# Activation-table preloads, norm order, scratch buffers and one-hot copies rearranged in an eight-core encoder step

## The chip, the cores and the metric

The kernel runs on all eight cores of one Trainium2 chip, each core on its own eighth of the tokens, with no exchange between cores. The time is that of the slowest core in device microseconds, from one launch. A profile shows one execution on its slowest core: TensorE (PE, with its weight loads PEld), VectorE (DVE), ScalarE (ACT), GpSimd (POOL, which only issues the weight loads here) and SyncE (SP, which issues the other transfers). PEclk is the granted TensorE clock, 1.00 for 2.4 GHz and 0.50 for 1.2 GHz.

## The reference

Two layers of a streaming encoder. Layer 0 mixes tokens by a convolution module, layer 1 by grouped-query attention with a relative-position bias; each layer ends with a SwiGLU block. Every block reads a modulated RMSNorm of the residual stream.

```python
for i in range(DEPTH):
    mod = jax.nn.silu(c) @ p['w_mod'][i] + p['b_mod'][i]
    sh1, sc1, g1, sh2, sc2, g2 = jnp.split(mod, 6, axis=-1)
    h = modulate(rms_norm(x, p['norm_mix'][i]), sh1, sc1)
    ...                                   # conv_module (i = 0) or attention (i = 1) -> y
    x = x + g1[:, None, :] * y
    h = modulate(rms_norm(x, p['norm_ffn'][i]), sh2, sc2)
    x = x + g2[:, None, :] * swiglu(h, p['w_gu'][i], p['w_down'][i])
return rms_norm(x, p['norm_out']), ...

def modulate(h, shift, scale):
    return h * (1 + scale[:, None, :]) + shift[:, None, :]

# bias of attention: bucket of (key position - query position), one table of 32 buckets x 32 heads
b = jnp.take(table.astype(jnp.float32), bucket, axis=1)
```

## The kernel before

Channels lie on the 128 partitions in 16 chunks (KC), tokens on the free axis (1184 columns X, in three tiles of 384, 384 and 416; from attention on 1056 columns in three tiles of 352). The last tile also holds the 2 x 16 sample tokens, which have their own modulation, so each modulated write of it is three instructions (384 or 320, 16 and 16 columns). All weights stream through a ring of four 1 MB slots (`RING`): POOL issues a load when TensorE has released a slot.

The order on every engine is the order in which the Python code emits it; engines wait for each other by semaphores. The stages in order: norm and modulation blocks, pw1 with the convolution, pw2 (its first three weight blocks as a head that goes chunk by chunk), FFN 0, k/v projection, the attention bias, attention with the q projections, output projection wo, FFN 1, final norm.

**Norm.** While the last projection before a norm runs, ACT squares each finished chunk and TensorE sums the squares with a matrix of ones into PSUM. Then `rstd1(t)` makes 1/rms of tile t: one Ln and one Exp on ACT. `rstd` calls it for tile 0, `rest` for tiles 1 and 2. `apply(t, c0, c1)` writes the modulated norm HB chunk by chunk: DVE multiplies X by 1/rms into one of three scratch buffers `T1`, then ACT (Identity with scale and bias) or DVE itself (`tensor_scalar`, chunks with c % 5 == 4, in tile 2 also c % 5 == 1) writes HB. A buffer is free again when that second step is done.

**FFN head.** TensorE starts gate and up of the first three weight blocks on tile 0, chunk by chunk as HB comes, into six PSUM banks. `evac` empties a pair: Silu on ACT into a scratch buffer `SGF` (two), multiply on DVE. Tiles 1 and 2 follow on the same three blocks; their `apply` calls stand between the evacuations in the code, so ACT and DVE do them in that order. Only after tile 2 of a block is its ring slot released.

**k/v projection.** The same chunk-by-chunk form for three tiles, on the same PSUM banks, so a tile can start only when `k_evac` (ACT) and `v_evac` (DVE) of the tile before are done. Part of the next tile's `apply` stands before these evacuations, the rest behind. After the last apply, `load_consts` loads caches and one-hot tables into space that X held.

**Attention bias.** 18 units; 16 of them first copy a shifted one-hot window (96 x 2048 bf16) into one of two buffers `OHW`, then TensorE does 16 small matmuls with it, then DVE adds the mask. After each unit TensorE does half a tile of the first q projection (8 matmuls of 352 columns); after every second half ACT evacuates the tile. The copies alternate between ACT and DVE, and each is issued one unit ahead (`oh_build(u + 1)` behind the matmuls of unit u).

**Tables.** `table(func)` is a one-element activation into `DUM`. ACT holds the functions of one table set at a time; the compiler puts an ACT_TABLE_LOAD straight in front of an activation whose function is not there. The nine calls stand where the next function is not needed yet.

Of the kernel before, what the change touches and what calls it, by code (L numbers as in the profile page):

```python
# [13 lines left out]
KC = 16  # L14
# [66 lines left out]
def build_nc():  # L81
# [44 lines left out]
    with es:  # L126
# [18 lines left out]
        EPSC = sb("EPSC", (128, 1), F32)  # L145
        DUM = sb("DUM", (128, 1), F32)
        BDW = sb("BDW", (128, 128), F32)
# [20 lines left out]
        XP = carve(UBraw, 9728, (128, KC, 32), F32)  # L168
        SGF = carve(SCR, 0, (128, 2, 416), F32)
        RSTD = carve(SCR, 3328, (128, NX), F32)  # L170
# [4 lines left out]
        T1U = carve(UBraw, 4736, (128, 3, 416), F32)  # L175
        YS = carve(UBraw, 4736, (128, 4, NQ), F32)
# [225 lines left out]

        def table(func):
            act(DUM[:], EPSC[:], func)

        sqf = [None, None, None]
        SB = (2, 4, 5)

        class Norm:
            def __init__(self, tiles):  # L410
                self.tiles = tiles
                self.k = 0
                self.pend = []
                self.cn = [0, 0, 0]
                self.ready = {}
                self.rtok = {}
                self.t1f = [None] * 3
                self.tk = 0
# [33 lines left out]
            def rstd(self, R, T, li, which):  # L452
                self.flush(0)
                self.R, self.T, self.li, self.which = R, T, li, which
                if which is not None:
                    tam = am_calc(li, which, 0, KC)
                    ACT.wait(tam)
                    DVE.wait(tam)
                    self.hb = {}
                self.rstd1(0)  # L460

            def rest(self):
                self.rstd1(1)
                self.rstd1(2)

            def apply(self, t, c0=0, c1=KC):
# [4 lines left out]
                for c in range(c0, c1):  # L471
                    i = self.tk % 3
                    self.tk += 1
                    Tc = self.T[:, i, :]
                    DVE.wait(self.t1f[i])
                    DVE.emit(nc.vector.tensor_tensor(out=Tc[:, 0:ncols], in0=X[:, c, xlo:xlo + ncols],  # L476
                                                     in1=self.R[:, xlo:xlo + ncols], op=ALU.mult))
                    td = DVE.tick()
                    if c % 5 == 4 or (t == 2 and c % 5 == 1):
                        DVE.wait(td)  # L480
                        for (a, b_, bi) in segs(xlo, xlo + ncols):
                            DVE.emit(nc.vector.tensor_scalar(
                                out=HB[:, c, 32 + a:32 + b_], in0=Tc[:, a - xlo:b_ - xlo], scalar1=AM[:, c, bi:bi + 1],
                                scalar2=MOD[:, li, sh0 + c, bi:bi + 1], op0=ALU.mult, op1=ALU.add))
# [86 lines left out]
        def ffn(li, tiles, nm, nm2):  # L571
            ngrp = (NFF + GRP - 1) // GRP
            sgf = [None] * 2
            st = {"kk": 0, "dk": 0, "sg": 0}

            def evac(j, t, bg, bu, tpg, tpu):
                xlo, ncols = tiles[t]
                aslot = (j // GRP % 2) * GRP + j % GRP
                i = st["sg"] % 2
                st["sg"] += 1  # L580
# [52 lines left out]
            for G in range(ngrp):  # L633
# [430 lines left out]
        t_bv = dma(SP, BVB, bkv_d.partition_broadcast(128), ldc_sem)  # L1064
        nm2.apply(0, 0, 3)
        nm2.rest()
        nm2.apply(0, 3, KC)
        table(AF.Exp)
        DVE.emit(nc.vector.memset(V1[:].rearrange("p v (g d) -> p v g d", d=65)[:, :, :, 64:65], 1.0))
        for t in range(3):  # L1070
# [463 lines left out]
```

How the kernel before makes its waits and increments, by code:

```python
    def tick(self):  # L61
        if not self.marked:
            self.n += 1
            self.last.then_inc(self.sem, 1)
            self.marked = True
        return (self.sem, self.n)
# [1 line left out]
    def wait(self, *ts):  # L68
        for t in ts:
            if t is None:
                continue
            sem, v = t
            if v <= 0:
                continue
            k = id(sem)
            if self.seen.get(k, 0) >= v:
                continue
            self.e.wait_ge(sem, v)
            self.seen[k] = v
# [166 lines left out]
        def dma(engw, out, in_, sem):  # L246
            engw.e.dma_start(out=out, in_=in_).then_inc(sem, 16)
            cnt[id(sem)] = cnt.get(id(sem), 0) + 1
            return (sem, 16 * cnt[id(sem)])
```

## Time and profile before

| | |
|---|---|
| Profiled execution, time | 3382.72 us |
| its span on the slowest core | 3381.0 us |
| spans of the eight cores | 3332.6 to 3381.0 us |
| three runs, median (lowest to highest) | 3572.45 us (3382.72 to 3860.07) |
| busy: PE / DVE / ACT / POOL | 2986.7 / 1147.8 / 708.6 / 187.2 us |
| mean granted clock of that core | 0.959 |

The profiled execution is the lowest of the three runs, and all durations below are its own. A line of the timeline is: start, duration, engine, source line, instruction, tiles and shapes, count of merged instructions, and in brackets how long the engine had been idle and on whom it waited. All TensorE instructions come from one helper, L252, all activations from L255; stages are told apart by tile names (SCR holds T1, SGF and the squares; UBraw holds T1 of the k/v norm and QT; Xraw holds X, and during attention the bias and one-hot tiles).

### The profile page before, as it was taken

The page shows a single profiled execution, that of the slowest core. Times are in us where ns is not written, and L with a number is a line of the kernel's source. Part 1 is how long each engine was busy: PE and PEld are TensorE (multiplying, and loading weights), DVE is VectorE, ACT ScalarE, POOL GpSimd, SP SyncE. Part 2 cuts the span into 40 slices and gives each one's busy share as a digit, 9 for nine tenths or more (in the row PEclk, how much of TensorE's full clock was granted, in tenths as well). Part 3 has the DMA queues.
Part 4 walks back from the last instruction along what each step waited for, and adds up shares of the span by engine and source line. Part 5 has one row for each costly group of instructions (what it writes and reads, how often), then busy time and mean ns, then how long its engine had stood idle before and what let it go on. Part 6 is the DMA issues. An engine that isn't in the chain of part 4 may idle for free.

```text
span 3381.0 us, 54942 instructions; the slowest of 8 cores (3332.6 to 3381.0 us)
## 1 busy us (share of the span) xinstructions
PE 2986.7 (88%) x21988; PEld 1855.3 (55%) x21988; DVE 1147.8 (34%) x2680; ACT 708.6 (21%) x1342; POOL 187.2 (6%) x357
## 2 busy tenths in 40 slices
PE   2299774688999999999999879889999999999996
PEld 0166453354556555565555447655556666666663
DVE  0345444614141221414122656633222222222236
ACT  2411111555000000000000556655200000000003
POOL 0000000000000000000000000000000000000000
PEclk9999886898999999999999989989999999999998
DMA  9789988593856566574523738653465253535243
GB/s 216 134 158 180 149 151 172 130 180 53 135 101 113 96 111 115 91 126 87 99 44 66 170 55 140 124 141 63 83 118 100 48 92 55 94 51 99 45 76 120
DMA packets 107976, 370.52 MB, mean 110 GB/s; under 512 B 31520, under 2 KB 51104, under 8 KB 78784
## 3 DMA queue, kind: packets, MB, share of 16 engines
q0 software_dynamic: 51024, 285.67, 49.4%
q1 hardware_dynamic: 56704, 81.34, 8.7%
q8 instruction: 180, 2.95, 0.4%
q14 instruction: 68, 0.56, 0.1%
HBM read 615.89 MB, written 33.78 MB: 192 GB/s over the span
## 4 chain that ended last, share of the span: by engine, by line
PE 77%; DMA 11%; DVE 5%; ACT 3%; issue 2%; SPq 1%; POOL 0%; DVEq 0%; ACTq 0%; POOLq 0%
PE ps L252 77%; DMA UBraw<-ud 2%; DMA ud<-UBraw 2%; ACT HBraw L255 1%; DMA Xraw<-xT 1%; SPq L247 1%; DMA RING<-wgu 1%; DMA RING<-wmod 1%; DMA zd<-UBraw 1%; ACT SCR L255 1%; DVE SCR L476 1%; DMA RING<-wpw 1%; DVE Xraw L663 1%; DVE Xraw L965 1%; DMA SCR<-bkv 0%
## 5 line engine op out<-in xcount | busy, mean ns | idle before, releaser
L252 PE MATMUL ps<-HBraw,RING 128*128 128x352 bf16 (+2 forms) x11616 | 1935.6, 327 | 84.9 <-ACT SCR L255 26.6
L252 PEld LDWEIGHTS ps<-HBraw,RING 128*128 128x128 bf16 x11616 | 1135.7, 99 | 815.3 <-issue 123.3
L252 PE MATMUL ps<-UBraw,RING 128*128 128x352 bf16 (+2 forms) x4992 | 813.9, 320 | 14.6 <-DVE UBraw L585 6.4
L252 PEld LDWEIGHTS ps<-UBraw,RING 128*128 128x128 bf16 x4992 | 472.8, 98 | 332.1 <-issue 64.6
L585 DVE TENSOR_TENSOR UBraw<-ps,SCR 128x352 bf16<-128x352 f32 (+2 forms) x264 | 144.2, 547 | 1181.5 <-PE ps L252 1172.6
L255 ACT ACTIVATE SCR<-ps 128x352 f32<-128x352 f32 (+2 forms) x264 | 127.0, 482 | 1823.7 <-PE ps L252 1822.9
L663 DVE SCALAR_TENSOR_TENSOR Xraw<-ps,MOD,Xraw 128x16 f32<-128x16 f32 (+3 forms) x960 | 395.3, 447 | 321.8 <-PE ps L252 321.8
L252 PE MATMUL ps<-SCR,ONESB 128*128 128x352 bf16 (+2 forms) x240 | 77.5, 363 | 84.6 <-ACT SCR L255 84.6
L252 PE MATMUL ps<-SCT,RING 128*128 128x3 bf16 x3072 | 90.6, 165 | 65.3 <-ACT HBraw L255 45.5
L252 PEld LDWEIGHTS ps<-SCT,RING 128*128 128x128 bf16 x3072 | 90.5, 97 | 78.0 <-issue 68.7
L255 ACT ACTIVATE SCR<-Xraw 128x352 bf16<-128x352 f32 (+2 forms) x190 | 107.5, 568 | 104.0 <-DVE Xraw L513 55.5
L252 PE MATMUL ps<-UBraw 128*128 128x156 bf16 x640 | 56.1, 257 | 69.3 <-DMA UBraw<-ud 66.9
L513 DVE TENSOR_TENSOR Xraw<-Xraw,SCR 128x352 f32<-128x352 f32 (+2 forms) x78 | 42.3, 542 | 182.7 <-ACT SCR L255 182.7
L247 POOL DMA_DIRECT2D RING<-wmod x96 | 50.9, 531 | 942.1 <-PE ps L252 932.2
L255 ACT ACTIVATE Xraw<-Xraw 128x512 bf16<-128x512 f32 (+4 forms) x146 | 93.2, 656 | 42.9 <-DVE Xraw L1243 34.8
L247 POOL DMA_DIRECT2D RING<-wdn x96 | 50.7, 528 | 861.2 <-PE ps L252 843.0
L247 POOL DMA_DIRECT2D RING<-wgu x88 | 46.5, 529 | 890.3 <-PE ps L252 887.6
L255 ACT ACTIVATE SCR<-ps,G1B,MOD 128x384 f32<-128x384 f32 (+3 forms) x160 | 79.1, 536 | 76.5 <-PE ps L252 64.0
L252 PEld LDWEIGHTS ps<-UBraw 128*128 128x128 bf16 x640 | 53.8, 110 | 72.7 <-issue 71.3
L1243 DVE SCALAR_TENSOR_TENSOR Xraw<-ps,Xraw 128x512 f32<-128x512 f32 x128 | 82.2, 685 | 31.4 <-PE ps L252 31.3
L252 PEld LDWEIGHTS ps<-SCR,ONESB 128*128 128x128 bf16 x240 | 23.3, 102 | 117.4 <-issue 109.4
L255 ACT ACTIVATE SCR<-UBraw 128x32 bf16<-128x32 f32 (+3 forms) x50 | 32.0, 639 | 245.2 <-DVE UBraw L857 190.6
(93 smaller groups left out, 1074.6 us busy)
## 6 DMA issues: line engine op xcount, KB each, us to landing
RING<-wmod POOLq DMA_DIRECT2D x96, 1024.0 KB, 13.2
RING<-wgu POOLq DMA_DIRECT2D x88, 1024.0 KB, 9.2
RING<-wdn POOLq DMA_DIRECT2D x80, 512.0 KB, 5.3
RING<-wpw POOLq DMA_DIRECT2D x24, 1024.0 KB, 17.1
Xraw<-xT SPq DMA_DIRECT2D x26, 592.0 KB, 11.9
RING<-wqkv POOLq DMA_DIRECT2D x10, 1024.0 KB, 14.3
zd<-UBraw SPq DMA_DIRECT2D x16, 592.0 KB, 10.1
Xraw<-zd SPq DMA_DIRECT2D x16, 592.0 KB, 7.6
```

Source lines behind the costliest of these rows:

```text
L247: engw.e.dma_start(out=out, in_=in_).then_inc(sem, 16)
L252: return PE.emit(nc.tensor.matmul(out, lhsT=lhsT, rhs=rhs, start=start, stop=stop, **kw))
L255: return ACT.emit(nc.scalar.activation(out=out, in_=in_, func=func, **kw))
L476: DVE.emit(nc.vector.tensor_tensor(out=Tc[:, 0:ncols], in0=X[:, c, xlo:xlo + ncols], in1=self.R[:, xlo:xlo + ncols], op=ALU.mult))
L513: DVE.emit(nc.vector.tensor_tensor(out=dst[:, xlo:xlo + ncols], in0=dst[:, xlo:xlo + ncols], in1=TMPE[:, 0:ncols], op=ALU.add))
L585: DVE.emit(nc.vector.tensor_tensor(out=ACTR[:, aslot, xlo:xlo + ncols], in0=PS[bu][:, 0:ncols], in1=SGF[:, i, 0:ncols], op=ALU.mult))
L663: DVE.emit(nc.vector.scalar_tensor_tensor(out=X[:, n, a:b_], in0=PS[bk][:, a - xlo:b_ - xlo], scalar=MOD[:, li, 80 + n, bi_:bi_ + 1], in1= ...
L965: DVE.emit(nc.vector.tensor_tensor(out=zt, in0=zt, in1=mv, op=ALU.subtract))
L1243: DVE.emit(nc.vector.scalar_tensor_tensor(out=SS[:, 2 * w + half, :], in0=bank[:, :], scalar=0.125, in1=BIAS[:, 8 * a + 2 * ip + half, :], ...
```

## The change

It touches five things; weights, matmuls and transfers stay, and the orders of PE, POOL and SP are the same row for row.

1. The nine `table` calls go.
2. `rest` goes: `rstd` makes 1/rms of all three tiles before the first `apply`.
3. `T1` has two buffers instead of three, `SGF` three instead of two. DVE writes HB itself for chunks with c % 4 == 3 in every tile.
4. The cuts of `apply` are moved: 8 and 8 chunks around the evacuations in FFN (10 and 6 before) and in k/v (3 and 13 before).
5. All one-hot copies go to ACT, and each is issued in its own unit, not one ahead.

```diff
-        T1 = carve(SCR, 8064, (128, 3, 416), F32)
+        T1 = carve(SCR, 9728, (128, 2, 416), F32)
-        SGF = carve(SCR, 0, (128, 2, 416), F32)
+        SGF = carve(SCR, 0, (128, 3, 416), F32)
-        def table(func):
-            act(DUM[:], EPSC[:], func)
...
-                self.rstd1(0)
-            def rest(self):
-                self.rstd1(1)
-                self.rstd1(2)
+                for t in range(3):
+                    self.rstd1(t)
...
-                    i = self.tk % 3
+                    i = self.tk % 2
...
-                    if c % 5 == 4 or (t == 2 and c % 5 == 1):
+                    if c % 4 == 3:
...
-            nm.apply(0, 0, 3)
-            nm.rest()
-            nm.apply(0, 3, KC)
-            table(AF.Silu)
+            nm.apply(0)
...
-            nm.apply(1, 0, 10)
+            nm.apply(1, 0, 8)
             for j in range(3):
                 evac(j, 0, hbk[j][0], hbk[j][1], tp, tp)
-            nm.apply(1, 10, KC)
+            nm.apply(1, 8, KC)
...
             if t < 2:
-                nm2.apply(t + 1, 0, 3)
+                nm2.apply(t + 1, 0, 8)
...
-                nm2.apply(t + 1, 3, KC)
+                nm2.apply(t + 1, 8, KC)
...
-        def oh_build(u):
-            t, qg, x = u // 9, u % 9, ohs.index(u) % 2
...
-            if x:
-                DVE.wait(ohfree[x])
-                DVE.emit(nc.vector.tensor_copy(out=dst, in_=src))
-                oh_t[u] = DVE.tick()
-            else:
-                ACT.wait(ohfree[x])
-                act(dst, src, AF.Copy)
-                oh_t[u] = ACT.tick()
         def bias_unit(u):
...
             if qg < 8:
-                PE.wait(oh_t[u])
+                ACT.wait(ohfree[u % 2])
+                act(OHW[0:96, u % 2, :, :].rearrange("r q (p i) -> r q p i", p=8), src, AF.Copy)
+                PE.wait(ACT.tick())
...
-            if u + 1 in ohs:
-                oh_build(u + 1)
```

What stands in ACT's queue at the start of FFN 0, before (SCR<-ps,EPSC is an Ln, SCR<-SCR its Exp, HBraw<-SCR an apply, DUM the preload of Silu, SCR<-ps a Silu):

```order
L255 ACTIVATE SCR<-ps,EPSC 128x384
L255 ACTIVATE SCR<-SCR 128x384
L255 ACTIVATE HBraw<-SCR,MOD,AM 128x384 x3
L255 ACTIVATE SCR<-ps,EPSC 128x384
L255 ACTIVATE SCR<-SCR 128x384
L255 ACTIVATE SCR<-ps,EPSC 128x416
L255 ACTIVATE SCR<-SCR 128x416
L255 ACTIVATE HBraw<-SCR,MOD,AM 128x384 x10
L255 ACTIVATE DUM<-EPSC 128x1
L255 ACTIVATE HBraw<-SCR,MOD,AM 128x384 x8
L255 ACTIVATE SCR<-ps 128x384 x3
L255 ACTIVATE HBraw<-SCR,MOD,AM 128x384 x5
```

The same place in the changed kernel:

```order
L254 ACTIVATE SCR<-ps,EPSC 128x384
L254 ACTIVATE SCR<-SCR 128x384
L254 ACTIVATE SCR<-ps,EPSC 128x384
L254 ACTIVATE SCR<-SCR 128x384
L254 ACTIVATE SCR<-ps,EPSC 128x416
L254 ACTIVATE SCR<-SCR 128x416
L254 ACTIVATE HBraw<-SCR,MOD,AM 128x384 x18
L254 ACTIVATE SCR<-ps 128x384 x3
L254 ACTIVATE HBraw<-SCR,MOD,AM 128x384 x6
```

Two Ln and Exp pairs moved from behind the third apply to ahead of the first, the preload is gone, and six instead of eight applies of tile 1 stand before the Silus.

ACT's queue in the attention bias, before (Xraw<-Xraw 96x2048 is a one-hot copy, UBraw<-ps the evacuation of a q tile):

```order
L255 ACTIVATE Xraw<-Xraw 96x2048 x2
L255 ACTIVATE UBraw<-ps,VTs 128x352
L255 ACTIVATE Xraw<-Xraw 96x2048
L255 ACTIVATE UBraw<-ps,VTs 128x352
L255 ACTIVATE Xraw<-Xraw 96x2048
L255 ACTIVATE UBraw<-ps,VTs 128x352 x2
```

and in the changed kernel:

```order
L254 ACTIVATE Xraw<-Xraw 96x2048 x2
L254 ACTIVATE UBraw<-ps,VTs 128x352
L254 ACTIVATE Xraw<-Xraw 96x2048 x2
L254 ACTIVATE UBraw<-ps,VTs 128x352
L254 ACTIVATE Xraw<-Xraw 96x2048 x2
```

Two copies now stand between two evacuations where one stood; the other eight copies left DVE's queue.

## Rows read from the trace of the kernel before

**Rows 1.** The page, part 4: the chain that ended last, by engine.
```profile
PE 77%; DMA 11%; DVE 5%; ACT 3%; issue 2%; SPq 1%; POOL 0%; DVEq 0%; ACTq 0%; POOLq 0%
```

**Rows 2.** Windows: length, busy us (instructions) of each engine, PEclk, DMA share, GB/s.
```profile
786.00:836.00 50.00, 39.23 (x209) 20.89 (x209) 34.97 (x77) 36.06 (x70) 0.00 (x0) 0.88 0.12 22
1925.00:1987.00 62.00, 42.40 (x272) 24.45 (x272) 38.62 (x96) 42.38 (x84) 7.70 (x14) 0.86 0.47 95
1987.00:2019.00 32.00, 24.11 (x387) 17.62 (x388) 17.85 (x33) 16.18 (x14) 0.53 (x1) 0.87 0.48 91
2347.00:2395.00 48.00, 37.04 (x209) 21.12 (x210) 32.64 (x77) 33.91 (x70) 0.00 (x0) 0.87 0.10 20
```

**Rows 3.** Groups by line and form: count, busy us, mean ns, idle before.
```profile
L255 ACT ACTIVATE UBraw<-ps,VTs 128x352 bf16<-128x352 f32 x48 | 26.3, 548 | 31.0 <-PE ps L252 31.0
...
L255 ACT ACTIVATE Xraw<-Xraw 96x2048 bf16<-96x2048 bf16 x8 | 15.2, 1903 | 5.8 <-DMA UBraw<-cv 3.9 <-PE ps L252 1.9
...
L255 ACT ACT_TABLE_LOAD x10 | 12.8, 1283 | 25.4 <-DMA FLAG<-flag 14.2 <-DVE UBraw L939 9.7 <-PE ps L252 1.4
...
L1130 DVE COPY Xraw<-Xraw 96x2048 bf16<-96x2048 bf16 x8 | 5.8, 722 | 0.0
L482 DVE TENSOR_SCALAR HBraw<-SCR,AM,MOD 128x384 bf16<-128x384 f32 x12 | 5.7, 479 | 1.3
```

**Rows 4.** Timeline of ACT before pw2: LayerNorm statistics, then its application.
```profile
583.83 1.28 ACT L255 ACT_TABLE_LOAD   x1 [9.67 <-DVE UBraw L939]
...
591.44 0.71 ACT L255 ACTIVATE HBraw<-Xraw,VTs 128x384 bf16<-128x384 f32 x1 [0.43 <-DVE Xraw L967]
```

**Rows 5.** Timeline, start of FFN 0: 1/rms, first applies, first matmuls.
```profile
786.67 0.52 ACT L255 ACTIVATE SCR<-SCR 128x384 f32<-128x384 f32 x1
...
787.95 1.90 ACT L255 ACTIVATE HBraw<-SCR,MOD,AM 128x384 bf16<-128x384 f32 x3 [0.76 <-DVE SCR L476]
...
788.94 17.31 PE L252 MATMUL ps<-HBraw,RING 128*128 128x384 bf16 x96 [2.76 <-DVE SCR L476]
...
789.76 0.56 ACT L255 ACTIVATE SCR<-ps,EPSC 128x384 f32<-128x384 f32 x1
...
791.98 1.29 ACT L255 ACTIVATE HBraw<-SCR,MOD,AM 128x384 bf16<-128x384 f32 x2
```

**Rows 6.** Timeline, FFN 0 head: applies, first Silus, restarts of TensorE.
```profile
795.65 2.61 DVE L476 TENSOR_TENSOR SCR<-Xraw,SCR 128x384 f32<-128x384 f32 x5
796.30 2.50 ACT L255 ACTIVATE HBraw<-SCR,MOD,AM 128x384 bf16<-128x384 f32 x4 [0.61 <-DVE SCR L476]
...
807.06 0.84 ACT L255 ACTIVATE SCR<-ps 128x384 f32<-128x384 f32 x2
...
808.39 4.79 PE L252 MATMUL ps<-HBraw,RING 128*128 128x384 bf16 x15 [2.14 <-DVE UBraw L585]
...
814.02 14.73 PE L252 MATMUL ps<-HBraw,RING 128*128 128x384 bf16 x89 [0.83 <-ACT HBraw L255]
...
835.80 14.48 PE L252 MATMUL ps<-HBraw,RING 128*128 128x416 bf16 x70 [0.45 <-ACT HBraw L255]
```

**Rows 7.** Timeline, k/v: evacuation of tile 0, last apply, constants (POOL), first copy.
```profile
1940.87 2.35 ACT L255 ACTIVATE SCR<-ps,VTs 64x384 bf16<-64x384 f32 x4
...
1965.90 3.77 ACT L255 ACTIVATE HBraw<-UBraw,MOD,AM 128x384 bf16<-128x384 f32 x9 [0.96 <-DVE UBraw L476]
...
1970.28 4.11 POOL L247 DMA_DIRECT2D SCR<-ckT  x8 [51.44 <-ACT HBraw L255]
...
1985.14 1.91 ACT L255 ACTIVATE Xraw<-Xraw 96x2048 bf16<-96x2048 bf16 x1 [3.93 <-DMA UBraw<-cv]
```

**Rows 8.** Timeline, attention bias: a unit, its q matmuls, first matmuls of attention.
```profile
2004.12 0.55 PE L252 MATMUL ps<-Xraw 96*128 96x32 bf16 x16 [1.00 <-ACT Xraw L255]
...
2004.53 1.35 PE L252 MATMUL ps<-HBraw,RING 128*128 128x352 bf16 x8
...
2018.45 1.87 PE L252 MATMUL ps<-UBraw,SCR 128*128 128x256 bf16 x8 [1.48 <-DVE Xraw L1165]
```

More of the change, by code:

```diff
@@ L145, in build_nc @@
         EPSC = sb("EPSC", (128, 1), F32)
-        DUM = sb("DUM", (128, 1), F32)
         BDW = sb("BDW", (128, 128), F32)
@@ L168, in build_nc @@
         XP = carve(UBraw, 9728, (128, KC, 32), F32)
-        SGF = carve(SCR, 0, (128, 2, 416), F32)
-        RSTD = carve(SCR, 3328, (128, NX), F32)
-        T1 = carve(SCR, 8064, (128, 3, 416), F32)
+        SGF = carve(SCR, 0, (128, 3, 416), F32)
+        RSTD = carve(SCR, 4992, (128, NX), F32)
+        T1 = carve(SCR, 9728, (128, 2, 416), F32)
         SQ = carve(SCR, 13056, (128, 3, 416), BF16)
@@ L174, in build_nc @@
         RSTDU = carve(UBraw, 0, (128, NX), F32)
-        T1U = carve(UBraw, 4736, (128, 3, 416), F32)
+        T1U = carve(UBraw, 4736, (128, 2, 416), F32)
         YS = carve(UBraw, 4736, (128, 4, NQ), F32)
@@ L416, in __init__ @@
                 self.rtok = {}
-                self.t1f = [None] * 3
+                self.t1f = [None, None]
                 self.tk = 0
@@ L572, in ffn @@
             ngrp = (NFF + GRP - 1) // GRP
-            sgf = [None] * 2
+            sgf = [None] * 3
             st = {"kk": 0, "dk": 0, "sg": 0}
@@ L578, in evac @@
                 aslot = (j // GRP % 2) * GRP + j % GRP
-                i = st["sg"] % 2
+                i = st["sg"] % 3
                 st["sg"] += 1
@@ L643, in ffn @@
                 last = G == ngrp - 1
-                if last:
-                    table(AF.Ln)
                 PE.wait(DVE.tick())
@@ L706, in build_nc @@
         trs = ACT.tick()
-        table(AF.Sigmoid)
         DVE.wait(trs, t_ld)
@@ L946, in build_nc @@
         tstat = ACT.tick()
-        table(AF.Silu)
         DVE.wait(tstat)
@@ L1064, in build_nc @@
         t_bv = dma(SP, BVB, bkv_d.partition_broadcast(128), ldc_sem)
[L1065 to L1068, printed above, removed]
+        nm2.apply(0)
         DVE.emit(nc.vector.memset(V1[:].rearrange("p v (g d) -> p v g d", d=65)[:, :, :, 64:65], 1.0))
@@ L1118, in build_nc @@
         ohfree = [None, None]
-        ohs = [u for u in range(18) if u % 9 < 8]
-        oh_t = {}
-        def oh_build(u):
-            t, qg, x = u // 9, u % 9, ohs.index(u) % 2
-            src = OHP[0:96, qg, :, 0:16]
-            src = bass.AP(src.tensor, src.offset + 15 + 16 * t, [list(src.ap[0]), [-1, 16], [48, 8], [1, 16]])
-            dst = OHW[0:96, x, :, :].rearrange("r q (p i) -> r q p i", p=8)
-            if x:
-                DVE.wait(ohfree[x])
-                DVE.emit(nc.vector.tensor_copy(out=dst, in_=src))
-                oh_t[u] = DVE.tick()
-            else:
-                ACT.wait(ohfree[x])
-                act(dst, src, AF.Copy)
-                oh_t[u] = ACT.tick()
         def bias_unit(u):
@@ L1141, in bias_unit @@
             if qg < 8:
-                PE.wait(oh_t[u])
+                src = OHP[0:96, qg, :, 0:16]
+                src = bass.AP(src.tensor, src.offset + 15 + 16 * t, [list(src.ap[0]), [-1, 16], [48, 8], [1, 16]])
+                ACT.wait(ohfree[u % 2])
+                act(OHW[0:96, u % 2, :, :].rearrange("r q (p i) -> r q p i", p=8), src, AF.Copy)
+                PE.wait(ACT.tick())
             PE.wait(*bf[bk])
@@ L1145, in bias_unit @@
                 if qg < 8:
-                    oh = OHW[0:96, ohs.index(u) % 2, q, :]
+                    oh = OHW[0:96, u % 2, q, :]
                 else:
@@ L1151, in bias_unit @@
             if qg < 8:
-                ohfree[ohs.index(u) % 2] = tp
-            if u + 1 in ohs:
-                oh_build(u + 1)
+                ohfree[u % 2] = tp
             DVE.wait(tp)
@@ L1200, in build_nc @@
         gq = q_dense(0)
-        oh_build(0)
         for u in range(18):
@@ L1374, in build_nc @@
         nm4.rstd(RSTDU, T1U, 1, None)
-        nm4.rest()
         y_t = [None] * 4
```

2 lines of the change are left out of this document (removed).

## The prediction, as it was put on record

> **What bounds the kernel now.** I read the chain of waits first: TensorE holds 77% of it [rows 1], so work on ACT and DVE costs nothing except where TensorE waits for it. So I looked next for the stretches where it does, in the windows: the starts of the two FFNs, the k/v projection and the attention bias. There TensorE is busy 39 of 50, 37 of 48, 42 of 62 and 24 of 32 us, at a granted clock of 0.86 to 0.88 [rows 2]. The edits that are not free lie in these 192 us; the timelines of the stretches give the price. In the FFN start the reader should see three restarts of TensorE: at 788.94 behind the first apply, at 808.39 behind the first Silu, and at 814.02 and 835.80 behind the last applies of tiles 1 and 2 [rows 5, 6].
>
> **Table preloads.** A load takes 1.28 us, and there are ten [rows 3]. In the order of the code the functions change Silu, Ln, Sigmoid, Ln, Silu, Ln, Silu, Ln, Exp, Ln, Silu, Ln; that gives ten loads if Exp needs none behind Ln, nor Ln behind Exp, so the preloads of Exp and of Ln before FFN 1 load nothing, and on demand the same ten remain. A load without a preload begins only when the wait of its activation is over: at 583.83 ACT had stood 9.67 us for DVE, and then loaded [rows 4]. So each load whose activation heads the chain costs 1.28 us: the Ln of 1/rms at FFN 0, k/v and the final norm, and the first Silu of both FFN heads. Two others cost nothing. The Silu of pw2's LayerNorm falls on its first chunk, but a chunk there takes ACT 0.71 us of a cycle of 0.71 + 0.43 that DVE sets [rows 4], so ACT has made up 1.28 us after three chunks; without that slack it costs 1.28. The Sigmoid of pw1 is hidden while TensorE fills the other pair of banks (32 matmuls, over 5 us at the 0.166 us each of [rows 6]).
>
> The Trainium skill (ScalarE: Activation LUTs, What ACT_TABLE_LOAD costs) adds a drain of about 1.38 us to each load, 2.66 us in all. The trace shows only 1283 ns, and the load at 583.83 starts with ACT already idle; by the page these five loads would make the sum below 7 us longer.
>
> **FFN 0 head.** (a) The first apply begins after ACT's Exp, which ends at 787.19, and after DVE's multiply. In the change two Ln and Exp pairs stand ahead of it; from 789.76 to 791.98 they take 2.22 us [rows 5]. Behind the load ACT is free at about 787.1 + 1.28 + 2.22 = 790.6 instead of starting at 787.95: **+2.65**. TensorE's 96 matmuls follow by as much, if the applies keep up.
>
> (b) Do they, with two T1 buffers? Before, five chunks take ACT 2.50 + 0.61 us [rows 6], 0.62 a chunk. After: an apply of 0.70, 0.1 to DVE, a multiply of 0.55, 0.1 back: a buffer returns every 1.45 us. Of four chunks ACT starts the first at 0, the second at 0.6, the third at 1.45; DVE's multiply of the fourth waits for the second's buffer until 1.4, its own write (0.48, [rows 3]) ends at 2.5, the multiply behind it at 3.0, and ACT starts again at 3.1: 0.775 a chunk. TensorE takes 17.31 / 16 = 1.08 [rows 5]. So the head stays bound by TensorE and ends at 806.25 + 2.65 = 808.9.
>
> (c) The first Silu now carries its load, +1.28. Before, ACT came to it 0.8 us after the head had ended (807.06 against 806.25), since apply work and preload stood ahead; after, 24 chunks at 0.775 from 790.6 end at 809.2, so ACT arrives in time and wins that back: **+0.5**.
>
> (d) Behind the Silus eight chunks of tile 1 remain instead of six, at 0.775 instead of 0.62: 2.5 us more, of which TensorE's own first matmuls, at 0.32 us each after the 2.14 us wait [rows 6], cover some: **+1.9** (1.0 to 2.5). (e) Tile 2's applies are three instructions each. Three such chunks take ACT 3.77 us [rows 7], with a buffer handover about 4.8 us per four chunks. Against the 21.8 us between the restarts at 814.02 and 835.80, 16 chunks at 1.2 us plus two evacuations come to about 23: **+1.2**. Sum for FFN 0: +6.3 (4 to 8). FFN 1 has the same code on 352 columns, 48 us against 50 [rows 2], and no load of Ln: 6.3 x 48/50 - 1.3 = **+4.7**.
>
> Behind the heads no cover waits: a ring slot is released only after tile 2, and the next weight loads are issued by that release, so they slide along.
>
> **k/v.** The first apply slides by the same 2.65. Then ACT must finish eight chunks of the next tile, not three, before each evacuation of 2.35 us, which TensorE waits for on its banks. Adding ACT's work: before, 19 chunks at 0.62, the pairs 2.22, the evacuation, 16 more chunks (three of them of tile 2), the evacuation, 13 of tile 2 at about 1.07; after, 24 at 0.775, 2.35, 8 at 0.775 and 8 at 1.2, 2.35, 8 at 1.2. That is 43.9 us against 48.7, plus 2.65: +7.5 for the last apply; the actual end, 1969.67, is 1.5 us earlier than my sum gives, so I take **+6.5** (4.5 to 7.5). TensorE ends later by more, but what counts is the constants: POOL issues them when the last apply is done (1970.28), and the first copy at 1985.14 waits for them [rows 7], so the stage moves with the apply.
>
> **Attention bias.** A copy takes ACT 1.90 us, DVE 0.72 [rows 3]. After the change ACT has all 16: 16 x 1.90 + 6 evacuations x 0.55 = 33.7 us against 32 for the whole stretch [rows 2], and no copy can be started past an evacuation, which waits for TensorE. A pair of units becomes a chain: copy 1.90, handoff 0.1, the second copy (1.80 behind the first), matmuls 0.40, q matmuls 1.35 [rows 8], handoff 0.1, evacuation 0.55: 6.2 us instead of 3.2. From the first evacuation (ends near 1992.9): three pairs 18.6, the unit pair with one copy 4.3, one pair 6.2, the last five copies 9.1, the tail 2.1: attention starts at 2033.2 instead of 2018.45, **+14.7** at full clock. TensorE then idles about 2.4 us in each pair. After 2.14 us of idle the 15 matmuls at 808.39 took 0.32 us each, the 1.2 GHz level; after 1.00 us at 2004.12 the next eight still took 1.35, the 2.4 GHz level [rows 6, 8]. At 1.2 GHz the q matmuls of units 2 to 11 cost up to 7 us more: +22. A gap of 2.4 is nearer to 2.14: I take **+18** (14 to 22).
>
> **At nothing.** The third SGF buffer: in the main FFN loops ACT waits for TensorE. DVE's freed time in the bias: it waited for TensorE there too. The removed one-element activations: 0.2 us each, off the chain.
>
> **Sum.** 6.3 + 6.5 + 18 + 4.7 + 1.3 (the last Ln) = 36.8; 3382.7 + 36.8 = **3420 us**, 1.1% up. With the bounds of the terms it is 27 to 45 us. All this is against the profiled execution; the median of the runs shown, 3572.45, lies 5.6% above it and is no base for this sum.
>
> **Rivals.**
> - *Cover.* The delays are swallowed behind each stage. For it: the constants already bound k/v, and weight loads are waited for after both FFN heads. Against: those transfers are issued on release by the delayed work. If both FFN heads were swallowed, 36.8 - 11 = 26 remain: 3409.
> - *The clock falls and stays down in the heads.* (Ends slower.) More waits push TensorE to 1.2 GHz for the whole of the FFN heads and k/v. Two tiles of an FFN head, 32 x 3 matmuls at 0.166 each, then cost 16 us more; two heads 32, k/v about 8, with the bias at +22: 36.8 + 4 + 40 = 81, 3464, +2.4%. It passes 2% when the clock of the FFN windows, 0.88 now, falls to about 0.6. Against: at 814.02, 0.83 us after a wait, the clock was back up [rows 6]. The Trainium skill (TensorE: Matmul & The Clock Gate, HAM oscillation) describes such a kernel, where a wait in every tile made each start cold; our trace shows cold starts of some microseconds, not whole tiles.
> - *ACT hides it.* The compiler's loads land earlier than I think, and DVE's even share (4 chunks per tile, not 3, 3 and 6) keeps the pace: only the bias remains, 3400.
>
> **How the numbers follow.** Chances: my sum (3410 to 3428) 0.60, cover 0.13, ACT hides it or the bias is cheaper 0.10, clock 0.12, something that gains over all 0.05. The likeliest gives 3420. The range from **3390 to 3456** reaches down past the bias-only case, so that half of the 0.05 for a gain stays in, and up to where the clock case has done most of its harm; half of that case and the larger gains are left out. A measurement here tells about 2% (68 us) from no change: faster 0.03, same 0.84, slower 0.13; slower is the clock case and a little of my own upper end.
>
> **What would show it.** ACT_TABLE_LOAD still about ten times, directly ahead of Ln and Silu, with TensorE idle. First FFN 0 matmul about 2.7 us later behind the last ones-matmul; its first restart idle near 2.7 us, tile 2's last apply 6 us later. In the bias stretch ACT busy without gaps over its last units, pairs of 6 to 7 us, no DVE copy. Wrong would be: a bias stretch under 40 us, the loads hoisted, or a granted clock under 0.7 in the FFN heads.

## The result and the profile after

The changed kernel took **3409.59 us** (median of 4 executions, 3407.21 to 3411.13). Against the kernel before the ratio is **1.0087, 95% interval [1.0062, 1.0111]**: +29.5 us, interval 21 to 37.5, where the forecast was +36.8 (3420, range 3390 to 3456). Executions in which the cores of a die ran at a lower clock, as those of 3572 and 3860 us in the figures before, are left out here and below, and of two experiments (e1, e7) the profile is read on cores 4 to 7 alone, which were undisturbed. A second comparison later, with many more executions of the kernel before beside it, gave 1.0115 [1.0089, 1.0140], +38.9 us. The mean of the eight cores' spans, which does not hang on the one slowest core, grew by 37.0 us from the profiled execution of before to the four of the changed kernel (3359.9 to 3396.9), and by 44.4 in the second comparison (3357.9 over 10 executions, 3402.3 over 5).

The chain of waits by engine, after, answers to [rows 1]; ACT's share rose from 3 to 4%:

```profile
PE 78%; DMA 9%; DVE 4%; ACT 4%; issue 2%; SPq 1%; DVEq 0%; POOL 0%; ACTq 0%; POOLq 0%
```

Table loads by line and form, after (count, busy us, mean ns, idle before), against [rows 3]: still ten, still 1283 ns; the copies on ACT went from 8 to 16.

```profile
L254 ACT ACTIVATE Xraw<-Xraw 96x2048 bf16<-96x2048 bf16 x16 | 29.5, 1897 | 0.0
L254 ACT ACT_TABLE_LOAD x10 | 12.8, 1283 | 40.3 <-DMA FLAG<-flag 14.6 <-DVE UBraw L924 9.7 <-PE ps L251 8.0
```

Three of the four stretches as windows, after (length, busy us of each engine, granted clock, DMA share, GB/s): the bias stretch, FFN 0's head and k/v; they answer to [rows 2], where they took 32, 50 and 62 us at 0.86 to 0.88.

```profile
1990.70:2038.20 47.50, 26.39 (x385) 17.55 (x386) 12.75 (x24) 30.18 (x21) 0.53 (x1) 0.82 0.30 60
779.40:837.40 58.00, 42.31 (x208) 21.39 (x207) 35.21 (x73) 38.79 (x74) 0.00 (x0) 0.82 0.08 17
1922.40:1990.70 68.30, 45.40 (x272) 25.75 (x273) 38.77 (x91) 45.29 (x89) 7.70 (x14) 0.80 0.42 83
```

These are two single cores, before and after. TensorE's busy time rose by only some 2 to 3 us in each; the rest of the growth is TensorE standing.

**The start of FFN 0, after** (timeline; it answers to [rows 5, 6]):

```profile
779.43 1.28 ACT L254 ACT_TABLE_LOAD   x1 [0.46 <-issue]
780.72 0.58 ACT L254 ACTIVATE SCR<-ps,EPSC 128x384 f32<-128x384 f32 x1
...
784.05 1.29 ACT L254 ACTIVATE HBraw<-SCR,MOD,AM 128x384 bf16<-128x384 f32 x2
...
784.88 1.44 PE L251 MATMUL ps<-HBraw,RING 128*128 128x384 bf16 x4 [5.43 <-ACT HBraw L254]
...
802.62 1.28 ACT L254 ACT_TABLE_LOAD   x1 [0.83 <-PE ps L251]
...
805.28 3.27 PE L251 MATMUL ps<-HBraw,RING 128*128 128x384 bf16 x10 [2.74 <-ACT SCR L254]
```

A load stands directly ahead of the Ln and of the first Silu, and TensorE waits behind both. Ln begins 0.01 us after the load ends. TensorE's first matmul comes 5.45 us after ACT begins. Before, on core 1, it came 2.94 us after Ln began (788.94 in [rows 5] against the row below); on the seven other cores it was 2.80.

```profile
786.00 0.58 ACT L255 ACTIVATE SCR<-ps,EPSC 128x384 f32<-128x384 f32 x1 [0.47 <-issue]
```

**The time by stage, on all eight cores.** The time counts the slowest core, and this hides what the stages do. So I read on every core, in the timelines, when each stage begins: the first Ln of a 1/rms or the load ahead of it, the first down projection of each FFN, the first bias matmul, attention's first matmul, the end of the last row of the timeline. The table has means over the cores, in us.

| kernel | start to FFN 0's Ln (lowest and highest core) | to first down projection | to k/v's Ln | to first bias matmul | to attention | to FFN 1's Ln | to first down projection | to last Ln | to the end | sum from FFN 0's Ln |
|---|---|---|---|---|---|---|---|---|---|---|
| before | 770.2 (743.4 to 788.7) | 160.2 | 977.7 | 61.1 | 31.4 | 326.5 | 149.1 | 855.3 | 24.6 | 2585.9 |
| changed | 767.9 (758.2 to 779.4) | 166.6 | 977.7 | 68.4 | 49.2 | 327.2 | 155.4 | 855.0 | 26.7 | 2626.3 |
| changed, again | 776.4 (755.7 to 788.7) | 168.3 | 977.8 | 68.5 | 49.9 | 327.2 | 155.6 | 855.0 | 27.3 | 2629.5 |
| growth (first) | -2.3 | **+6.4** | 0.0 | **+7.3** | **+17.8** | +0.7 | **+6.3** | -0.3 | +2.1 | **+40.4** |

The two traces of the changed kernel differ by up to 1.7 us in a stage and 3.2 in the sum; less than that is not read from this table. From FFN 0's Ln to the end the eight cores of a kernel lie within 7 to 10 us of one another. Ahead of it they lie 21 to 45 us apart, and there no growth stands out of the spread (-2.3 and +6.2 us on the mean).

The largest part of that spread is one wait: it gives 22 of the 43 us between cores 1 and 2 before, and 19 of the 21 between cores 2 and 1 after. TensorE's waits from 100 to 800 us, that for the transfer of the gated convolution's input (total us, times, longest), first before on cores 1 and 2, its slowest and its fastest:

```profile
PE ps L252 <- DMA UBraw<-ud: 66.9, 4, 26.7
PE ps L252 <- DMA UBraw<-ud: 44.9, 5, 24.7
```

and after, on cores 2 and 1, again its slowest and its fastest:

```profile
PE ps L251 <- DMA UBraw<-ud: 73.3, 4, 23.4
PE ps L251 <- DMA UBraw<-ud: 53.9, 5, 26.5
```

Behind it everything is regular. First down projection of FFN 0 and the beginning of k/v's 1/rms, before, core 1 and then core 2:

```profile
947.46 2.76 PE L252 MATMUL ps<-UBraw,RING 128*128 128x384 bf16 x16 [0.53 <-DVE MOD L376]
1925.29 0.58 ACT L255 ACTIVATE UBraw<-ps,EPSC 128x384 f32<-128x384 f32 x1 [5.98 <-DVE AM L398]
902.74 2.44 PE L252 MATMUL ps<-UBraw,RING 128*128 128x384 bf16 x14 [0.53 <-DVE MOD L376]
1880.40 0.58 ACT L255 ACTIVATE UBraw<-ps,EPSC 128x384 f32<-128x384 f32 x1 [5.98 <-DVE AM L398]
```

and after, core 2:

```profile
944.63 2.60 PE L251 MATMUL ps<-UBraw,RING 128*128 128x384 bf16 x15 [0.53 <-DVE MOD L375]
1922.37 1.28 ACT L254 ACT_TABLE_LOAD   x1 [5.96 <-DVE AM L397]
```

1925.29 - 947.46 = 977.83, 977.66 and 977.74: two cores 45 us apart and two kernels, the same to 0.2 us.

### The profile page after: what moved, and what is told of

It is laid out like the page before. It is cut to its first block, busy times and chain, and to the rows that moved or that the text cites. A ratio compares the mean times of both kernels' runs of the same rounds, so it can differ in the third digit from the quotient of the medians.

```text
span 3406.0 us, 54951 instructions; the slowest of 8 cores (3391.6 to 3406.0 us)
## 1 busy us (share of the span) xinstructions
PE 2993.4 (88%) x21988; PEld 1858.2 (55%) x21988; DVE 1143.7 (34%) x2660; ACT 726.1 (21%) x1353; POOL 187.4 (6%) x357
## 4 chain that ended last, share of the span: by engine, by line
PE 78%; DMA 9%; DVE 4%; ACT 4%; issue 2%; SPq 1%; DVEq 0%; POOL 0%; ACTq 0%; POOLq 0%
PE ps L251 78%; DMA UBraw<-ud 2%; DMA ud<-UBraw 2%; ACT HBraw L254 2%; SPq L246 1%; DMA RING<-wgu 1%; DMA RING<-wmod 1%; DMA Xraw<-xT 1%; ACT SCR L254 1%; DMA zd<-UBraw 1%; ACT Xraw L254 1%; DMA RING<-wpw 1%; DVE Xraw L949 1%; DVE Xraw L649 0%; DVE UBraw L469 0%
## 5 line engine op out<-in xcount | busy, mean ns | idle before, releaser
L251 PE MATMUL ps<-HBraw,RING 128*128 128x352 bf16 (+2 forms) x11616 | 1938.5, 327 | 95.3 <-ACT HBraw L254 43.6
L251 PE MATMUL ps<-UBraw,RING 128*128 128x352 bf16 (+2 forms) x4992 | 812.5, 320 | 14.8 <-DVE UBraw L576 6.4
L254 ACT ACTIVATE Xraw<-Xraw 128x512 bf16<-128x512 f32 (+4 forms) x154 | 107.2, 720 | 38.0 <-DVE Xraw L1208 35.3
```

The source lines that it names most:

```text
L251: return PE.emit(nc.tensor.matmul(out, lhsT=lhsT, rhs=rhs, start=start, stop=stop, **kw))
L254: return ACT.emit(nc.scalar.activation(out=out, in_=in_, func=func, **kw))
```

## The experiments

Two theories: **the terms add up** (each edit has its price on every core, nothing is given back, and the slowest core's time blurs this by the draw of the wait ahead of FFN 0), and **cover** (about 10 us of the delays are given back in later waits on each core; this rival's 3409 is what was measured). Ratios are to the kernel before on the same chip.

**r_after: the changed kernel again, unedited.**

> The changed kernel once more, without any edit, beside many executions of the kernel before on one chip. The first comparison, +29.5 us, rests on two undisturbed executions of before (3377 and 3383), and the kernel before now shows executions from 3365 up. Theory 'the terms add up': the stage prices read on the eight cores sum to 40, the ratio is 1.010 to 1.012 (+34 to +41). Rival 'cover' (about 10 us are given back on each core): 1.0087 or less, +29.

Measured: median 3418.04 us, ratio 1.0115 [1.0089, 1.0140], +38.9 us (30 to 47); sum of the stages 2629.5. As the first theory says. This interval and that of the first comparison (21 to 37.5) overlap, and the cover rival's +29 lies just below this one.

**e1: the bias edit alone.**

```
 before, with
-        def oh_build(u): ...            # ACT and DVE in turn, one unit ahead
+                act(OHW[0:96, u % 2, :, :]..., src, AF.Copy)   # in bias_unit(u), all on ACT
+                PE.wait(ACT.tick())
```

> The kernel before with the bias edit alone: all 16 one-hot copies on ACT, each in its own unit. The stretch from the first bias matmul to attention's first matmul is 31.4 us on the mean of eight cores before and 49.2 us in the changed kernel. Theory 'the terms add up' (each edit has its own price on each core and nothing is given back): this stretch grows by 17 to 19 us on every core, no other stage moves by over 1 us, and the mean over the cores' spans grows by the same 18. The time of the slowest core then grows by 10 to 22, since the wait for the gated convolution's transfer (45 to 75 us, different on each core) sits ahead of it. Rival 'cover': the stretch grows by 18, but waits behind it (weights of wo, FFN 1) shrink, and the cores' spans grow by less than 14.

Measured: ratio 1.0069 [1.0044, 1.0093], +23 us. The bias stretch took 51.1 us (+19.7), k/v 60.7, attention 326.8, FFN 1's head 148.4, the sum 2605.3 (+19.4). Nothing behind it shrinks by more than 0.7 us: no cover. The stretch itself grew by a little more than the 17 to 19 that I gave.

**e2: the changed kernel with the bias code of before.** The reverse of e1.

```
 changed kernel, with
+        def oh_build(u): ...
+            if u + 1 in ohs:
+                oh_build(u + 1)
```

> The changed kernel with the one-hot copies of before put back (ACT and DVE in turn, one unit ahead). Theory 'the terms add up': from FFN 0's Ln to the end 2626 to 2630 less 18 to 19.5, so 2607 to 2611 on the mean of the cores, and the bias stretch back at 31.4. Rival 'cover': under 2603, since part of the delays of the other stages would be given back where the bias stretch no longer hides them.

Measured: ratio 1.0056 [1.0037, 1.0075]; bias stretch 31.1, sum 2607.1 (+21.2 on before, 19.2 below the changed kernel's first trace and 22.4 below its second). The bias edit is worth about 19 us from either side; within what two traces differ, its price does not depend on the other edits.

**e8: all copies on ACT, but issued one unit ahead.**

```
 before, with
-            if x:
+            if False:
```

> The kernel before with all 16 copies on ACT but still issued one unit ahead: the engine without the loss of the early issue. Per pair of units ACT has 2 x 1.90 + 0.55 = 4.35 us of work. If the early issue matters, the pair takes 4.4 to 4.9 us instead of 6.2 and the bias stretch 38 to 42 us, between 31.4 and the 49 to 51 of the full edit. If only the engine matters, it stays at 47 to 51.

Measured: bias stretch 37.9 us (+6.5), just under the range given. The total shows a ratio of 1.0001 [0.9984, 1.0019], which does not exclude those 5 to 6 us; the mean of the eight cores' spans shows them, 3363.9 over 7 executions against 3357.9 over 10, +6.0. A pair of units in e8 (timeline, its slowest core):

```profile
1987.00 3.70 ACT L255 ACTIVATE Xraw<-Xraw 96x2048 bf16<-96x2048 bf16 x2
1987.01 1.35 PE L252 MATMUL ps<-HBraw,RING 128*128 128x352 bf16 x8
...
1989.15 0.55 PE L252 MATMUL ps<-Xraw 96*128 96x32 bf16 x16 [0.79 <-ACT Xraw L255]
1989.55 1.35 PE L252 MATMUL ps<-HBraw,RING 128*128 128x352 bf16 x8
...
1991.00 0.55 ACT L255 ACTIVATE UBraw<-ps,VTs 128x352 bf16<-128x352 f32 x1 [0.30 <-PE ps L252]
```

and in the changed kernel (core 2):

```profile
1996.09 3.70 ACT L254 ACTIVATE Xraw<-Xraw 96x2048 bf16<-96x2048 bf16 x2
1998.13 0.55 PE L251 MATMUL ps<-Xraw 96*128 96x32 bf16 x16 [2.87 <-ACT Xraw L254]
1998.53 1.35 PE L251 MATMUL ps<-HBraw,RING 128*128 128x352 bf16 x8
...
2001.79 0.55 ACT L254 ACTIVATE UBraw<-ps,VTs 128x352 bf16<-128x352 f32 x1 [2.00 <-PE ps L251]
2002.24 3.70 ACT L254 ACTIVATE Xraw<-Xraw 96x2048 bf16<-96x2048 bf16 x2
2004.39 0.59 PE L251 MATMUL ps<-Xraw 96*128 96x32 bf16 x16 [2.70 <-ACT Xraw L254]
2004.82 2.51 PE L251 MATMUL ps<-HBraw,RING 128*128 128x352 bf16 x8
```

In both, ACT copies twice and evacuates once per pair. With the early issue ACT idles 0.30 us a pair and the copies run under TensorE's q matmuls: 4.45 us from pair to pair in the steady part (ACT begins to copy at 1987.00 and again at 1991.45). Without it ACT idles 2.00 us until the evacuation's matmuls are through, and TensorE 2.7 to 2.9 us until the copy is there: 6.15 us (1996.09 to 2002.24). Of the 18 us, some 6.5 are ACT's slower copy and 11 to 13 the lost early issue, taken in this order; late copies that ACT and DVE still share were not run.

**e7: all copies on DVE, one unit ahead.**

```
 before, with
-            if x:
+            if True:
```

> The kernel before with all 16 one-hot copies on DVE (0.72 us each instead of 1.90 on ACT), still issued one unit ahead. If TensorE waits in this stretch for ACT's copies (four waits of 1.0 to 2.2 us before), the bias stretch shrinks from 31.4 to 25 to 28 us and the mean of the cores' spans by 4 to 6; if DVE's additions and the q projection set the pace, it shrinks by less than 2.

Measured: bias stretch 28.5 (-2.9), ratio 0.9983 [0.9964, 1.0002]: less gain than I gave, at the interval's edge (the mean of the cores' spans fell by 4.5, 8 executions against 18). In the middle of the stretch TensorE no longer waits (timeline, core 5), but the second unit's q matmuls now run at the 1.2 GHz level too (2.51 us here; 1.35 to 2.15 on the cores of before), and at the end it waits for DVE's copies instead of ACT's:

```profile
1969.69 2.51 PE L252 MATMUL ps<-HBraw,RING 128*128 128x352 bf16 x8
...
1972.47 2.51 PE L252 MATMUL ps<-HBraw,RING 128*128 128x352 bf16 x8
...
1993.03 0.55 PE L252 MATMUL ps<-Xraw 96*128 96x32 bf16 x16 [1.10 <-DVE Xraw L1130]
...
1994.26 0.55 PE L252 MATMUL ps<-Xraw 96*128 96x32 bf16 x16 [0.67 <-DVE Xraw L1130]
```

**e3: the preloads removed, nothing else.**

```
 before, without the nine calls
-            table(AF.Silu)      # and table(AF.Ln), table(AF.Sigmoid), table(AF.Exp)
```

> The kernel before without the preloads of activation tables, nothing else. Theory of 1.28 us per exposed load: from Ln to the first matmul of FFN 0 and of k/v +1.3 each, final norm to the end +1.3; the Silu loads of the FFN heads keep their place behind the applies of tile 0 or fall into slack, 0 to +1 each; no exposed load ahead of FFN 1's Ln. In all +4 to +5 us on the mean of the cores. By a rule of 2.66 us per load, with a drain: +8 to +10 at the same places. Rival 'hidden': the loads are moved ahead by the compiler, 0.

Measured: ratio 1.0026 [1.0004, 1.0048]; sum 2591.6 (+5.7). Ln (or its load) to the first matmul: 4.10 on all eight cores at FFN 0 and at k/v, where before had 2.80 (2.94 on one core at FFN 0), and 2.67 as before at FFN 1. This is 1.3 a load, not 2.66. Last Ln to the end +1.0. The sum is a little over the 4 to 5 that I gave. The Silu loads were not as hidden as I expected; ACT of e3 (core 5) at the end of FFN 0's head:

```profile
788.35 2.50 ACT L255 ACTIVATE HBraw<-SCR,MOD,AM 128x384 bf16<-128x384 f32 x4 [0.61 <-DVE SCR L473]
792.25 1.28 ACT L255 ACT_TABLE_LOAD   x1 [1.39 <-PE ps L252]
```

ACT had been waiting 1.39 us for TensorE when the load began, so the load is wholly exposed; before, ACT came 0.8 us late to the same Silu, so by these two rows the net is about +0.5, as term (c) has it. FFN 0's stage grew by 3.0 in all, FFN 1's by 0.5; what 1.3 and 0.5 leave of the former is within two traces of one kernel.

**e4: order of 1/rms, buffers and cuts, without the other two edits.**

```
 changed kernel, with table(...) and oh_build(...) of before put back
```

> The changed kernel with the table preloads and the shared, early bias copies of before put back: what is left is 1/rms of all three tiles ahead of the first apply, two T1 buffers, three SGF buffers, DVE's even share, and the cuts 8/8. Theory 'the terms add up': Ln to first matmul +1.4 at FFN 0, FFN 1 and k/v; FFN 0 head in all +5, FFN 1 head +5.5, k/v +6; sum +16 to +17 on the mean of the cores, bias stretch unchanged at 31.4. Rival 'cover': FFN stages behind the heads shrink and the sum is under +10.

Measured: ratio 1.0040 [1.0024, 1.0055], +13.5 us; sum 2600.0 (+14.1): FFN 0 +4.4, k/v +5.3, FFN 1 +4.0, bias stretch 31.6. Ln to the first matmul +1.3, +1.4 and +1.2. Somewhat under my 16, above cover's 10. The three parts alone give 19.4 + 5.7 + 14.1 = **39.2**, the whole 40.4 and 43.6: they add up. The means of the cores' spans say the same without a trace, 18.9 + 7.5 + 16.1 = 42.5 against 44.4.

**e5: three T1 buffers in the changed kernel** (SGF back to two, for room).

```
-        SGF = carve(SCR, 0, (128, 3, 416), F32)
-        T1 = carve(SCR, 9728, (128, 2, 416), F32)
+        SGF = carve(SCR, 0, (128, 2, 416), F32)
+        T1 = carve(SCR, 8064, (128, 3, 416), F32)
...
```

> The changed kernel with three T1 buffers (and two SGF buffers) as before. Theory: the pace of the applies, 0.78 us a chunk with two buffers, makes terms (d) and (e) and part of k/v: first matmul to first down projection 161.2 to about 158.5 in FFN 0 and 151.5 to 149 in FFN 1, k/v (first matmul to first bias matmul) 62.7 to about 60; in all -6 to -9. Rival: the cuts 8/8 and the order of 1/rms make them, and the buffers change less than 2 in all.

Measured: ratio 1.0067 [1.0036, 1.0097]; sum 2614.8, 11.5 to 14.7 below the changed kernel, more than I expected. k/v 62.2 (-6.2), FFN 1 151.4 (-4.0), FFN 0 165.2 (-1.4). So the lost buffer is most of the price of k/v (6.2 of 7.3) and of FFN 1 (4.0 of 6.3) and a small part of FFN 0's (1.4 of 6.4); the rival, under 2 in all, is out. What the SGF buffer that went back adds or hides here was not run apart. ACT in k/v, changed kernel (core 2):

```profile
1930.37 1.30 ACT L254 ACTIVATE HBraw<-UBraw,MOD,AM 128x384 bf16<-128x384 f32 x2 [0.94 <-DVE UBraw L469]
1931.83 0.71 ACT L254 ACTIVATE HBraw<-UBraw,MOD,AM 128x384 bf16<-128x384 f32 x1 [0.16 <-DVE UBraw L469]
1933.48 1.30 ACT L254 ACTIVATE HBraw<-UBraw,MOD,AM 128x384 bf16<-128x384 f32 x2 [0.94 <-DVE UBraw L469]
```

and with three buffers (e5, core 3):

```profile
1935.37 1.90 ACT L254 ACTIVATE HBraw<-UBraw,MOD,AM 128x384 bf16<-128x384 f32 x3 [0.61 <-DVE UBraw L469]
1937.89 1.90 ACT L254 ACTIVATE HBraw<-UBraw,MOD,AM 128x384 bf16<-128x384 f32 x3 [0.61 <-DVE UBraw L469]
```

Four chunks (three by ACT, one by DVE) begin 3.11 us apart with two buffers and 2.52 with three. At 0.59 a group the twelve groups of k/v's three tiles make 7 us, about the 6.2 that it lost.

**e6: k/v's cut 3/13 in the changed kernel.**

```
-                nm2.apply(t + 1, 0, 8)
+                nm2.apply(t + 1, 0, 3)
```

> The changed kernel with the k/v cut 3/13 in place of 8/8. Theory 'ACT's sum sets the last apply' (as in the prediction): the same work in another order, k/v from its first matmul to the first bias matmul stays within 1 us of 62.7. Rival 'the cut itself holds TensorE's banks': it falls by 3 to 4, to about 59.

Measured: the time has no interval (two executions, 3406 and 3415); k/v from its first matmul 61.5 against 62.7, hardly outside my 1 us, far from the rival's 59. But what ends the stage changes. With 3/13 the first copy waits for the constants' transfer, by 1.4 to 4.8 us on the eight cores (e6, core 3):

```profile
1989.28 1.51 ACT L254 ACTIVATE SCR<-ps,VTs 64x384 bf16<-64x384 f32 x4 [7.09 <-PE ps L251]
...
1996.49 3.71 ACT L254 ACTIVATE Xraw<-Xraw 96x2048 bf16<-96x2048 bf16 x2 [3.28 <-DMA UBraw<-cv]
```

With 8/8 it does not (changed kernel, core 2): ACT waits 11.96 us for TensorE's last k/v matmul, evacuates, and goes through its exponentials straight into the first copy, which the trace groups with them as x4; it is so on all eight cores.

```profile
1974.04 4.12 POOL L246 DMA_DIRECT2D SCR<-ckT  x8 [58.11 <-DVE HBraw L475]
...
1984.85 1.51 ACT L254 ACTIVATE SCR<-ps,VTs 64x384 bf16<-64x384 f32 x4 [11.96 <-PE ps L251]
...
1988.47 3.91 ACT L254 ACTIVATE Xraw<-Xraw 128x32 f32<-128x32 f32 x4
```

**e9: the kernel before with what the runs point to.**

```
-                    if c % 5 == 4 or (t == 2 and c % 5 == 1):
+                    if c % 4 == 3:
-                nm2.apply(t + 1, 0, 3)
+                nm2.apply(t + 1, 0, 8)
-            if x:
+            if True:
```

> The kernel before with three edits that the runs point to: all one-hot copies on DVE, one unit ahead (bias stretch 28.5 instead of 31.4); DVE's even share of every fourth chunk, with three T1 buffers kept; k/v cut 8/8. Preloads, order of 1/rms and the FFN cut 10/6 stay. If the even share is what made k/v 56.7 with three buffers even behind a late 1/rms, k/v goes from 58.3 to about 55 and the sum from FFN 0's Ln to the end falls by 4 to 8 us from 2586, ratio 0.997 to 0.9985. If the constants' transfer sets k/v's end, k/v stays near 57 and only the bias gain of 3 is left.

Measured: ratio 0.9982 [0.9963, 1.0001], median 3364.14; sum 2580.2, 5.7 below before. The bias stretch gives 3.0, FFN 1's head 1.9, FFN 0's and k/v only 1 each (k/v 60.2, not the 58 that I looked for). From its first matmul k/v took 57.4, near the 57 that I gave for the transfer's case, yet the transfer does not set it: it had landed 2.1 to 5.0 us before the first copy on every core. What holds k/v there was not followed up. It beats both kernels by its stages, and the changed kernel clearly; against the kernel before the total's interval just reaches no change.

## Where the prediction was right, and where it failed

**The base of the sum: the step that failed.** The sum was 3382.7 + 36.8: the slowest core's time of one execution, plus the terms, as if that core's lead over the others stayed as it was. It is a draw. In the profiled execution of before the slowest core lay 21.1 us above the mean of its eight (3381.0 against 3359.9), in the four executions of the changed kernel only 8.0 to 13.2. The mean of the eight grew by 37.0, where the terms sum to 36.8 (the means of single executions scatter by 2 to 5 us); so no term was given back, and what +29.5 lacks is the smaller lead. The base was high as well: later executions of before average 3372.4, 3378.4 and 3372.9 (18, 10 and 13 of them; the lowest 3364.7). In the two profiles the slowest core of before ends its stages at 786.0 + 2591.5 us, that of the changed kernel at 779.4 + 2623.0. The 25 us between them are -6.6 from ahead of FFN 0 and +31.5 behind it, and there before's core 1 is the longest of its eight (mean 2585.9) and the other's core 2 among the shorter (mean 2626.3). What makes the wait for the convolution's transfer 45 us on one core and 75 on another was not tried, so why one execution draws higher stays open. The prediction also took a measurement to tell only 2% (68 us) from no change; the interval is some 8 us to either side. Within the sum two steps failed, FFN 1's clock and the path that ends k/v, both below.

**Cover**, the rival whose 3409 was hit, is refuted by the stages: 977.7 us behind FFN 0's head and 855 behind FFN 1's in every kernel, no shrinkage in e1 or e2, parts that sum to the whole. That 3409 was measured is luck.

**Preloads: right.** Ten loads, where the prediction put them, none hoisted; 1.3 us at each exposed Ln. The Trainium skill (ScalarE: Activation LUTs, What ACT_TABLE_LOAD costs) has about 2.66 us with a drain of 1.38. No run here shows a drain: Ln began 0.01 us behind the load at 779.43, and e3's way from Ln to the first matmul grew by 1.3. The measurement decides.

**FFN 0: right, in part by luck**, 6.4 and 8.1 against 6.3. First matmul +2.6 against 2.65; four chunks 3.11 us apart against 3.1; first restart idle 2.74 against "near 2.7". But TensorE's waits for tile 1 grew by 1.15 us where (d) has 1.9, and its run behind them (89 or 90 matmuls) by 1.4 on the mean of the cores, for which the sum has no term: more of it fell to the 1.2 GHz level.

**FFN 1: mis-sized**, 6.3 and 6.5 against 4.7. The step that failed is the clock in the heads, which the sum puts at nothing because it was back up at 814.02. TensorE's first restart of the head, its run behind the waits for tile 1, and its last restart, before (core 2):

```profile
2319.54 1.65 PE L252 MATMUL ps<-HBraw,RING 128*128 128x352 bf16 x10 [1.44 <-DVE UBraw L585]
...
2324.91 13.44 PE L252 MATMUL ps<-HBraw,RING 128*128 128x352 bf16 x89 [0.80 <-ACT HBraw L255]
...
2345.18 2.21 PE L252 MATMUL ps<-HBraw,RING 128*128 128x352 bf16 x7 [0.44 <-ACT HBraw L255]
```

and after (core 2):

```profile
2387.85 1.35 PE L251 MATMUL ps<-HBraw,RING 128*128 128x352 bf16 x8 [2.68 <-ACT SCR L254]
...
2394.29 16.34 PE L251 MATMUL ps<-HBraw,RING 128*128 128x352 bf16 x90 [0.38 <-ACT HBraw L254]
...
2418.58 1.79 PE L251 MATMUL ps<-HBraw,RING 128*128 128x352 bf16 x5 [0.68 <-ACT HBraw L254]
```

From the first of these restarts to the last as windows, before and after (length, busy us of each engine, granted clock, DMA share, GB/s):

```profile
2319.54:2345.18 25.64, 18.46 (x112) 10.70 (x113) 17.25 (x45) 16.41 (x39) 0.00 (x0) 0.98 0.00 1
2387.85:2418.58 30.73, 22.73 (x110) 11.60 (x111) 17.27 (x41) 18.76 (x45) 0.00 (x0) 0.75 0.00 1
```

The run took 13.44 us on seven cores of before (14.64 on core 1, where the first restart came after 2.83 us of idle instead of 1.4 to 1.7), and 16.3 on five and 14.8 to 14.9 on three of the changed kernel: +2.2 on the mean. The other terms came out as forecast or lower: first restart +1.6 against 1.7, waits for tile 1 +1.1 against (d)'s 1.8, those for tile 2 +1.2 against (e)'s 1.2 (each scaled by 48/50). Three buffers (e5) take 4.0 off this stage, out of the waits.

**k/v: size right by luck, path wrong.** +7.3 against 6.5. I let the constants' transfer end the stage and called TensorE's later end hidden. It is TensorE that ends it under the cut 8/8 (e6's rows). Counted from Ln, on the mean of the cores, the last apply moved from 45.3 to 50.5 us and the transfer's landing from 58.7 to 63.9, +5.2 each; TensorE's last k/v matmul moved from 52.3 to 62.4, +10.1. With the 3.9 us of evacuations and exponentials behind it, it now comes after the transfer, where before it came ahead of it. The two ways come out about equally long, so the sum did not suffer. The trace of before had the transfer as the last releaser on seven of its eight cores, and I did not work TensorE's new end out against it.

**Bias: right.** +17.8 and +18.5 against 18, by the chain of 6.2 us a pair (6.15 measured). The clock's part shows core by core: in the changed kernel the stretch is 47.4 us on the cores where two units' q matmuls took 2.5 us (one or two in before), 49.6 to 51.3 where four did, on some cores with two more between the levels. So the chain is 15 to 16 us, against my 14.7, as the second of the two slow units is counted to the clock or not, and the rest, up to 4, is the clock, against up to 7.

**The clock in the heads.** It fell from 0.88 to 0.82 in FFN 0's and from 0.86 to 0.80 in k/v's window, and not towards 0.6: matmuls at the 1.2 GHz level behind the waits, as the 15 of [rows 6]. From these means TensorE was at that level for some 12 us of 50 before and 21 of 58 after in FFN 0's head. The Trainium skill (TensorE: Matmul & The Clock Gate, HAM oscillation) describes cold starts in every tile. The trace agrees for the changed kernel: some of its bias units start cold, at about 1.2 us each, and in FFN 1's head every one of the three tiles starts with 3 to 10 us at the lower level; but no tile runs at it as a whole.

**At nothing: as said, but for the clock in the heads.** Attention and both long FFN parts moved by under 1 us. The end took 2.1 and 2.7 us more against 1.3, within what two traces of one kernel differ.

## What to carry to other kernels

Where a wait ahead of the change differs by tens of microseconds from core to core, read a change of one per cent by stage on every core: the stages tell 3 us where the slowest core's time tells 5 to 10. The mean of the cores' spans over all executions is a check that needs no trace. In this short pipeline between two engines the early issue was worth more than the faster engine: moving the copies to ACT cost 6.5 us, issuing them in their own unit 11 to 13 more. A buffer taken from a two-engine handover shows as a longer period per group of chunks (3.11 against 2.52 us), and the price is about that times the groups wherever TensorE waits for their end. And longer waits in front of TensorE can come with a lower clock behind them, as in FFN 1's head, where the run took 16.3 us instead of 13.4.

## What was not expected of the hardware

Eight cores with the same program and no exchange spent 45 to 75 us in the waits for one DMA round trip (44.9 on core 2, 75.4 on core 7 before), and later ran 977.7 us alike to 0.2 us. And within one kernel, behind idle times of 2.7 to 2.9 us alike, a unit's eight q matmuls took 1.35 us in one place and 2.51 in the next, so that the same stretch took 47.4 us on one core and 51.2 on another.
